# Softmax of the one-tile score banks: minima subtracted on VectorE, one exponential per bank on ScalarE, head sums on VectorE

## What is computed

```python
def masked_softmax(s, mask):
    s = jnp.where(mask, s.astype(jnp.float32), NEG_INF)
    m = jnp.max(s, axis=-1, keepdims=True)
    e = jnp.where(mask, jnp.exp(s - m), 0.0)
    return e / jnp.maximum(jnp.sum(e, axis=-1, keepdims=True), 1e-30)
...
        ps = masked_softmax(ss, pos_s <= t[:, None]).reshape(...)
        o_slc = jnp.einsum('bhgqnk,bhqnkd->bhgqd', ps.astype(vg.dtype), vg)
...
        pwin = masked_softmax(jnp.einsum('bhgqd,bhkd->bhgqk', qb, kwb), mw)
        o_win = jnp.einsum('bhgqk,bhkd->bhgqd', pwin.astype(vwb.dtype), vwb)
```

## Time and profile before

| | |
|---|---|
| time, median of 3 runs | 1400.08 us (1399.67 to 1400.54) |
| profiled execution, device time | 1401.01 us |
| profiled execution, span of its instructions | 1399.1 us |
| mean granted TensorE clock | 0.99 of full |
| TensorE busy | 1363.3 us (97%) |
| VectorE busy | 713.3 us (51%) |
| ScalarE busy | 606.3 us (43%) |
| GpSimd busy | 700.1 us (50%) |
| DMA, mean | 91 GB/s |

### The profile page before, as it was taken

The page is one execution under the profiler, slowest core; times in us unless marked ns, Lnnn a source line. Parts: engine busy times, 40 slices in busy tenths (PEclk is TensorE's granted clock), DMA queues, the critical chain, the costliest instruction groups (busy, mean ns, idle before and its releaser), DMA issues.

```text
span 1399.1 us, 17721 instructions
## 1 busy us (share of the span) xinstructions
PE 1363.3 (97%) x6904; PEld 1122.8 (80%) x6904; DVE 713.3 (51%) x900; ACT 606.3 (43%) x1087; POOL 700.1 (50%) x544
## 2 busy tenths in 40 slices
PE   8999988999999999999999999989999999999998
PEld 5889866778888888888888887767788888888886
DVE  5406556745544544644462075566355445556443
ACT  4233565756434333433442336656454333343322
POOL 2544775745444444544464456757435444445441
PEclk9999998999999999999999999989999999999999
DMA  5433420022333333333233333100323333333231
GB/s 202 136 100 106 131 65 16 1 91 91 105 91 97 99 93 103 90 103 93 61 121 112 108 106 119 31 16 2 121 68 115 104 91 104 93 96 100 90 106 61
DMA packets 34883, 127.19 MB, mean 91 GB/s; under 512 B 3952, under 2 KB 4464, under 8 KB 34416
## 3 DMA queue, kind: packets, MB, share of 16 engines
q1 hardware_dynamic: 34656, 125.53, 29.2%
q10 hardware_dynamic: 144, 0.52, 0.1%
HBM read 123.94 MB, written 2.10 MB: 90 GB/s over the span
## 4 chain that ended last, share of the span: by engine, by line
PE 89%; ACT 5%; DVE 3%; issue 1%; POOL 1%; DMA 0%; DVEq 0%; POOLq 0%; ACTq 0%; SPq 0%
PE bank L1719 33%; PE bank L1372 17%; PE bank L1751 17%; PE bank L1388 5%; PE bank L1616 3%; PE bank L1654 2%; PE bank L1677 2%; PE bank L1678 1%; ACT E L813 1%; PE bank L1562 1%; PE bank L1563 1%; PE bank L1476 1%; PE bank L1583 1%; PE bank L1340 1%; POOL w_lo L546 1%
## 5 line engine op out<-in xcount | busy, mean ns | idle before, releaser
L546 POOL TENSOR_TENSOR w_lo<-raw,w_hi 128x1024 fp32r<-128x1024 f32 x216 | 521.3, 2419 | 468.4 <-ACT w_hi L643 468.1
L643 ACT ACTIVATE w_hi<-raw 128x1024 fp32r<-128x1024 f32 x220 | 230.9, 1054 | 241.9 <-DMA raw<-wstream 241.8
L1719 PE MATMUL bank<-act_hi,w_hi 128*128 128x512 f32 (+1 forms) x768 | 286.0, 372 | 0.6 <-DVE act_lo L926 0.6
L1719 PE MATMUL bank<-act_hi,w_lo 128*128 128x512 f32 (+1 forms) x768 | 285.2, 371 | 0.0
L1719 PE MATMUL bank<-act_lo,w_hi 128*128 128x512 f32 (+1 forms) x768 | 285.2, 371 | 0.0
L885 ACT ACTIVATE cv<-bank,par 128x512 f32<-128x512 f32 x88 | 68.6, 779 | 286.0 <-PE bank L1719 286.0
L1301 DVE SCALAR_TENSOR_TENSOR cv<-bank,par,cv 128x511 f32<-128x511 f32 x88 | 66.0, 750 | 225.3 <-ACT cv L885 225.3
L1719 PEld LDWEIGHTS bank<-act_hi,w_hi 128*128 128x128 f32 x768 | 144.7, 188 | 26.9 <-DVE act_lo L926 1.6
L1719 PEld LDWEIGHTS bank<-act_hi,w_lo 128*128 128x128 f32 x768 | 144.7, 188 | 25.2
L1719 PEld LDWEIGHTS bank<-act_lo,w_hi 128*128 128x128 f32 x768 | 144.7, 188 | 24.7
L1372 PE MATMUL bank<-w_hi,act_hi 128*128 128x512 f32 (+1 forms) x384 | 144.5, 376 | 0.6 <-DVE w_lo L926 0.5
(11 more groups left out here) (175 smaller groups left out, 2231.9 us busy)
## 6 DMA issues: line engine op xcount, KB each, us to landing
raw<-wstream SPq DMA_DIRECT2D x220, 512.0 KB, 3.6
g_all<-gains SPq DMA_DIRECT2D x2, 2048.0 KB, 7.0
x_out<-x SPq DMA_DIRECT2D x8, 256.0 KB, 2.0
x<-x_in SPq DMA_DIRECT2D x3, 512.0 KB, 9.3
const<-consts SPq DMA_DIRECT2D x1, 1030.0 KB, 13.7
g_all<-gains ACTq DMA_DIRECT2D x1, 512.0 KB, 5.1
x<-x_in SPq DMA_DIRECT2D x2, 256.0 KB, 5.2
par<-pars SPq DMA_DIRECT2D x2, 235.0 KB, 3.5
```

Source lines behind the costliest of these rows:

```text
L546: nc.gpsimd.tensor_tensor(w_lo[:, s, :], raw_slot(s), r32(w_hi[:, s, :]), ALU.subtract)\
L643: nc.scalar.activation(w_hi[:, s, :], raw_slot(s), ACT.Copy).then_inc(hi_ready, 1)
L1719: last = mm(bank[:, b, first:end], a, v, start=(k == 0 and n == 0), stop=(k == KD - 1 and n == 2), skip_group_check=True)
```

## The change

For the units with i = 0 (`LOWERED`: 6, 7, 14, 15 of each layer) the subtraction of the minimum leaves the exponential. Right behind the minima of such a job, VectorE subtracts `s_bias` (broadcast over the columns) from all four heads of the bank and writes the result to `E`. ScalarE then takes one exponential over 128x512, in place in `E`, without bias and without the accumulator. Two items after the scores VectorE adds up the four heads' rows into `s_sum` with one reduction, and GpSimd's scaling waits for that (`summed`) and not for `e_done`. All other units are as before.

```diff
@@ -307,6 +308,9 @@
         e_done = sem("e_done", G * NU)
+        LOWERED = [n for n in range(NU) if UNITS[n][0] == 0]
+        lowered = sem("lowered", len(LOWERED))
+        summed = sem("summed", len(LOWERED))
...
@@ -599,7 +602,10 @@
-                    pool.wait_ge(e_done, upto(e_done, l, EXP_NO[n, 2 * p + 1]))
+                    if n in LOWERED:
+                        pool.wait_ge(summed, upto(summed, l, LOWERED.index(n) + 1))
+                    else:
+                        pool.wait_ge(e_done, upto(e_done, l, EXP_NO[n, 2 * p + 1]))
...
@@ -801,6 +807,11 @@
                     width = P * (UNITS[n][0] + 1)
+                    if n in LOWERED:
+                        act.wait_ge(lowered, upto(lowered, l, LOWERED.index(n) + 1))
+                        e = E[:, slot, :, col:col + width]
+                        nc.scalar.activation(e, e, ACT.Exp, scale=-1.0).then_inc(e_done, G)
+                        return
...
@@ -1191,6 +1202,22 @@
                         .then_inc(m_step, 1)
+                    if n in LOWERED:
+                        slot, col = E_AT[n]
+                        dve.wait_ge(m_step, upto(m_step, l, z + 1))
+                        dve.wait_ge(pt_done, upto(pt_done, l, last_turn(E_AFTER[n]) + 1))
+                        nc.vector.tensor_tensor(E[:, slot, :, col:col + width],
+                                                bank[:, S_BANK(z), :].rearrange("p (q c) -> p q c", q=G),
+                                                s_bias[:, n % SB, :].unsqueeze(2).broadcast_to([P, G, width]),
+                                                ALU.subtract).then_inc(lowered, 1)
+
+                def sums(n):
+                    slot, col = E_AT[n]
+                    dve.wait_ge(e_done, upto(e_done, l, EXP_NO[n, G - 1]))
+                    if n >= SB:
+                        dve.wait_ge(rec_done, upto(rec_done, l, PAIR_NO[n - SB, 1] + 1))
+                    nc.vector.tensor_reduce(out=s_sum[:, n % SB, :], in_=E[:, slot, :, col:col + P], axis=AXX,
+                                            op=ALU.add).then_inc(summed, 1)
...
@@ -1275,6 +1302,9 @@
                         minima(z)
+                    for z in jobs_at(k - 2):
+                        if JOBS[z][0] in LOWERED:
+                            sums(JOBS[z][0])
                     if k == Q7_AT + 8:
                         queries_rest(7)
```

More of the change, by code:

```diff
@@ L291, in build @@
         NU = T * NKV * 2
+        UNITS = [(i, g, b) for g in range(NKV) for i in reversed(range(T)) for b in range(2)]
         JOBS = [(n, r, 1) for p in range(2) for n in range(4) for r in (2 * p, 2 * p + 1)]
@@ L345, in build @@
         WO_CHUNK_AT = {1: C_WO + 1, 8: C_WO + 2, 17: C_WO + 3, 27: C_WO + 4, 33: C_WO + 5}
-        UNITS = [(i, g, b) for g in range(NKV) for i in reversed(range(T)) for b in range(2)]
         query_tile = lambda v: (T - 1 - v % T, v // T)
```

## The result

The changed kernel took **1402.76 us** (median of 20 runs, 1399.78 to 1404.43) against 1400.2 us for the kernel before in the same comparison (20 runs, 1398.19 to 1402.22): a ratio of 1.0015, interval 1.0009 to 1.0022. That is slower, by about 2.1 us, and less than the 0.2% that I had set as the line to no change. The forecast was 1401.0, range 1399.2 to 1402.8. Direction and class were right; the size was a good half short. The median lies inside the range by 0.04 us only, and in the band that I had given to a fall of the clock (chance 0.13), not in the forecast's own (1400.5 to 1401.9).

A forecast was written before the change was run, and what follows sets the result against it. TensorE, busy 97% of the span, was taken as the bound, so only its waits count. Added waits of 0.27 + 0.66 = +0.93 us on the 1400.08 us median gave 1401.0 us, range 1399.2 to 1402.8.

The forecast's parts named there:

- a fall of the clock: Band above the forecast's own, up to 1402.9 us, for one half-rate stretch of TensorE; chance 0.13.
- Which waits matter: TensorE's retention transposes wait for VectorE's query rest (3.6 us per layer) and splits (4.8 us together); units 6, 7 feed these.
- The price of each operation: Per unit: subtraction 0.69 us (slot 0.72), sum 0.68 (slot 0.60), exponential 0.63; VectorE gains 1.32 us of work.
- k = 9: Unit 6, query rest: ScalarE's copy 0.27 us earlier, sum in a 0.60 us slot, so TensorE's stall shrinks 0.15 us per layer.
- k = 11 and 13: Unit 7, second and third retention transposes: later by 0.36 then 0.27 us net in layer one, 0.06 then 0.66 in two.
- the 0.33 us that p_rest(12) was to win: First layer, item 12: VectorE's p_rest starts 0.33 us earlier because ScalarE's shorter exponential no longer holds out_sum.
- Hidden parts: GpSimd's scaling waits for the sums at no cost; unit 15's ends near 301, needed at 304.91, about 4 us cover.
- Sum: Added TensorE waits of both layers: 0.27 + 0.66 = +0.93 us, put on the median of the kernel before.
- my upper bound of +2.3: Subtraction and sum both land whole in both layers: 2 x 1.32 - 0.3 = +2.3 us.
- Hidden: Rival: the sum at k = 12 finds idle VectorE time, giving 1399.8 to 1400.4 us; chance 0.22.
- Clock: Rival: second layer's stall, grown from 1.30 to 1.9 us, drops TensorE to half rate, losing 1.7 us: 1402.7; chance 0.13.
- Faster: Rival: ScalarE's 0.83 us counts fully at k = 9: 1398.4 us (chance 0.05), or 1396.7 with the clock (0.03).

The follow-up runs named there:

- e2: The change made only in units 6 and 7 of each layer, 14 and 15 as in the kernel before: 1402.42 us, ratio 1.0012.
- e3: The change made only in units 14 and 15 of each layer, 6 and 7 as in the kernel before: 1400.88 us, ratio 1.0002.
- e13: e3 with the unread filling matmuls of e9 in TensorE's waits: 1391.32 us, ratio 0.9939.
- e4: Changed kernel with item 10's retention split ahead of minima and subtraction, and all sums behind query rest and split: 1399.83 us, ratio 0.9991.
- e6: Changed kernel with only the sums moved, behind the query rest (item 9) and the retention split (item 12): 1399.87 us, ratio 0.9994.
- e10: e4 with the unread filling matmuls of e9 in TensorE's waits: 1392.21 us, ratio 0.9935.
- e9: Kernel before, with 512-column matmuls whose results nobody reads put into TensorE's waits at items 1, 9, 13 and 15: 1391.39 us, ratio 0.9931.
- e11: Changed kernel (all four units) with the unread filling matmuls of e9 in TensorE's waits: 1394.54 us, ratio 0.9962.
- e1: The kernel before, unchanged, run again: 1400.48 us, ratio 0.9998.

## Why the prediction was right, and where it was short

- **Which waits matter: right.** Units 6 and 7 carry nearly the whole cost (e2), units 14 and 15 alone none (e3, e13), and the cost goes when the new work stands behind the splits and the query rest (e4, e6). With the clock held it goes only in part: e10 is 0.8 us above e9.
- **The price of each operation: right.** Subtraction 0.69 and sum 0.68 us, slots of 0.72 and 0.60. The exponential in place took 0.61.
- **k = 9: the step failed, by 0.15 us per layer.** The copy came 0.25 us earlier (223.59 less the trace's 0.89; forecast 0.27), but the sum and the query rest stood 0.71 us apart, not 0.60, and p_rest started 0.05 later than forecast. The gain was 0.01 to 0.02. That it was there to be had, e6 shows: 0.23 us once the sum is behind.
- **k = 11 and 13: right for the traces in sum.** As distances from the first transposes to the third, with item 9's gain in them, the forecast was +0.42 and +0.81, together 1.23; the traces show +0.62 and +0.55, together 1.17. The new wait in the first layer is 0.58 us (forecast half a microsecond), and the second layer's stall 1.89 (forecast 1.9). How it divides was off. In the first layer the 0.33 us that p_rest(12) was to win did not come: it stands 10.34 us behind the first transposes for 10.31 before. TensorE was 0.67 us late at its second transposes where 0.51 was forecast, and so released item 12's copy later. In the second layer p_rest(12) came no later (10.96 us for 11.00), since half rate ended earlier there than in the trace before, and of the shift only the sum was left. What the forecast lacks against the traces is thus item 9's gain, 0.93 for 1.2.
- **Hidden parts: right for the scaling, but two terms of about 0.3 us were put at nothing.** Unit 15's cover held. The two waits outside the loops, where a ScalarE instruction starts 0.28 us late once all four units are lowered, are in no term of the sum; I had priced ScalarE's shorter list as a gain or as nothing.
- **Sum: mis-sized.** Forecast 0.93, measured 2.1. Item 9's gain (0.3) that did not come and the two waits (0.5) bring it to 1.8. Besides, the forecast priced the waits at one clock phase, that of one trace. With TensorE held at full rate the new work is paid whole, 0.72 + 0.60 per layer, above my upper bound of +2.3 by the 0.3 gain that was not there: e11 shows 2.6 in its loops against e13. That the last 0.3 us come from runs between those phases is argued, not shown: no trace of a run with the full cost and without the fill was seen, and the runs sorted by clock do not bear it out, since the change lost nothing in its four runs at 0.990. That the median still fell into the range is luck: the band around 1402.76 had been given to a fall of the clock, and that is not what the runs show.
- **Rivals.** *Hidden* is refuted by e2. *Clock*: its point does not exist as a fixed length, since 1.90 us fell in e2 and not in the changed kernel, and the mean clock stayed equal; that the clock sets what the change costs in a given run stays possible. *Faster* is refuted by the unchanged 3.60 us.

## What to carry to other kernels

When an edit adds work to an engine with half its time idle, ask what stands behind it in that engine's list at the few places where the bounding engine waits: here the same work was worth +2 us ahead of the splits and nothing behind them (with the clock held, 3.2 and 0.8 us). When the bounding engine's rate varies from run to run, price the wait at its full rate as well as at the rate of the one trace. And a bounding engine that waits for some microseconds may lose more by its clock afterwards than by the wait: fill such waits first, and measure small edits with them filled, where the spread is 0.3 to 1 us and not 4. Compare with a kernel of the same comparison, and subtract the two traces instruction by instruction: the steps show waits that a list of the longest ones hides.

## What the hardware showed that I had not expected

- Stalls of 3.6 us of TensorE were each followed by half rate, those of 1.9 us in some traces and not in others, and those of 1.3 us at the retention transposes in none that I read. Work without use in those waits gave back 9.3 us in 1400.
- The spread of run times (1398 to 1402 us) is that clock: filled kernels, at five runs each, spread over 0.3 to 1.0 us.
- Stalls and clock trade against each other: in e1 half rate up to item 11 cut the stall at item 13 from 1.99 to 1.31 us.
- VectorE started the query rest 0.71 us behind a sum on which it does not depend, while minima or copies follow one another in 0.60.
- With 56 instructions fewer in ScalarE's list, one of its instructions per layer started 0.28 us late, in every trace of such a kernel, at the same two places; with 28 fewer, none did there.
